# A two-block model on one core: matmuls of a recurrence spread over the array's four quarters, and four smaller edits of order

## The reference

```python
for l in range(DEPTH):                       # DEPTH = 2
    h = rmsnorm(x, norm1_g[l])
    p = h @ w_in[l]
    y_rw = rwkv7_branch(p_rw, ...)           # the recurrence
    y_ret = retention_branch(p_ret, cos, sin)
    y_sg = sgu_branch(p_sg, ...)
    ...
    x = x + jnp.sum(gates * proj, axis=2) @ w_out[l]
    x = x + conv_ffn(rmsnorm(x, norm2_g[l]), ...)
```

```python
# S_t = S_{t-1} (diag(w_t) - kk_t^T (a_t * kk_t)) + v_t^T k_t ;  y_t = S_t r_t
kk = kk / jnp.maximum(jnp.sqrt(jnp.sum(kk * kk, axis=-1, keepdims=True)), 1e-12)
```

```python
mixed = jnp.concatenate([rms_norm(c, conv_out_g[l]), rms_norm(a, attn_out_g[l])], axis=-1)
x = x + mixed @ w_out[l]
```

## Time and profile before

| | |
|---|---|
| median of 3 runs | 2949.22 us (2946.46 to 2950.34) |
| profiled execution, its time | 2951.45 us |
| its span in the profile | 2949.6 us |
| PE busy | 2849.4 us, 97% |
| DVE, ACT, POOL busy | 1443.0, 1100.2 and 1091.7 us |

### The profile page before, as it was taken

The page is one execution under the profiler, slowest core; times in us unless marked ns, Lnnn a source line. Parts: engine busy times, 40 slices in busy tenths (PEclk is TensorE's granted clock), DMA queues, the critical chain, the costliest instruction groups (busy, mean ns, idle before and its releaser), DMA issues. The chain is left out here.

```text
span 2949.6 us, 45829 instructions
## 1 busy us (share of the span) xinstructions
PE 2849.4 (97%) x19056; PEld 2164.1 (73%) x19057; DVE 1443.0 (49%) x1780; ACT 1100.2 (37%) x1609; POOL 1091.7 (37%) x627
## 2 busy tenths in 40 slices
PE   8998999999999999899999999999989989999997
PEld 7877878888888877797888888877767755444543
DVE  6276423468762526642336887259865231222223
ACT  5573242343332448324234333255564331111112
POOL 4264244445444436414444444434434230010000
PEclk9999999999999999999999999999989989999999
DMA  5220022222232422102222222222223147999995
GB/s 186 69 86 24 11 103 86 95 93 100 93 106 91 137 72 83 38 4 90 107 88 86 100 100 102 99 99 84 85 72 104 58 185 289 407 416 415 414 410 240
DMA packets 59194, 407.65 MB, mean 138 GB/s; under 512 B 9073, under 2 KB 9841, under 8 KB 19057
## 3 DMA queue, kind: packets, MB, share of 16 engines
q1 hardware_dynamic: 58992, 404.82, 36.5%
HBM read 397.45 MB, written 2.10 MB: 135 GB/s over the span
## 5 line engine op out<-in xcount | busy, mean ns | idle before, releaser
L1219 POOL TENSOR_TENSOR back_w_lo<-w,back_w_hi 128x1024 fp32r<-128x1024 f32 (+1 forms) x240 | 542.0, 2267 | 637.9 <-ACT back_w_hi L1380 637.7
L1380 ACT CAST back_w_hi<-w 128x1024 fp32r<-128x1024 f32 (+1 forms) x240 | 229.7, 957 | 511.4 <-PE bank L1235 502.9
L1230 PE MATMUL bank<-h_hi,back_w_hi 128*128 128x512 f32 x1072 | 268.5, 392 | 1.5 <-DVE back_made_lo L1565 1.5
L1235 PE MATMUL bank<-h_hi,back_w_lo 128*128 128x512 f32 x1072 | 264.7, 389 | 0.0
L1232 PE MATMUL bank<-h_lo,back_w_hi 128*128 128x512 f32 x1072 | 264.7, 389 | 0.0
L292 POOL TENSOR_TENSOR front_w_lo<-w,next_hi 128x1024 fp32r<-128x1024 f32 x68 | 178.3, 2625 | 225.4 <-ACT next_hi L476 225.4
L1230 PEld LDWEIGHTS bank<-h_hi,back_w_hi 128*128 128x128 f32 x1072 | 201.1, 188 | 47.4 <-issue 3.8
L1232 PEld LDWEIGHTS bank<-h_lo,back_w_hi 128*128 128x128 f32 x1072 | 201.2, 188 | 41.8
L1235 PEld LDWEIGHTS bank<-h_hi,back_w_lo 128*128 128x128 f32 x1072 | 201.2, 188 | 41.7
L3183 PE MATMUL bank<-moe_w,moe_hg 128*64 128x512 f32 x1024 | 226.1, 594 | 0.2 <-DMA moe_w<-in_moe_w 0.2
L1985 POOL TENSOR_TENSOR mid_w_lo<-w,mid_w_hi 128x1024 fp32r<-128x1024 f32 x60 | 149.1, 2489 | 188.9 <-ACT mid_w_hi L2436 188.5
(11 more groups left out here) (596 smaller groups left out, 5779.9 us busy)
## 6 DMA issues: line engine op xcount, KB each, us to landing
moe_w<-in_moe_w SPq DMA_DIRECT2D x128, 1024.0 KB, 13.3
moe_w<-in_moe_w SPq DMA_DIRECT2D x32, 2048.0 KB, 12.5
w<-in_ffn_up SPq DMA_DIRECT2D x44, 1024.0 KB, 4.8
w<-in_w_merge SPq DMA_DIRECT2D x22, 1536.0 KB, 6.2
w<-in_w_in SPq DMA_DIRECT2D x30, 1024.0 KB, 4.8
w<-in_w_mid SPq DMA_DIRECT2D x29, 1024.0 KB, 4.9
w<-in_ffn_down SPq DMA_DIRECT2D x16, 1408.0 KB, 6.0
w<-in_w_out SPq DMA_DIRECT2D x16, 512.0 KB, 4.0
```

The source lines that it names most:

```text
L1219: nc.gpsimd.tensor_tensor(split(B.w_lo, n), raw(n), split(B.w_hi, n).bitcast(F32), ALU.subtract).then_inc(f["w_lo"], 1)
L1230: nc.tensor.matmul(bank, B.w_hi[:, n % 2, k, :], x_hi[:, cols], start=start and k == 0, stop=False)
L1235: mm = nc.tensor.matmul(bank, B.w_lo[:, n % 2, k, :], x_hi[:, cols], start=False, stop=stop and k == len(hi) - 1)
L1380: nc.scalar.copy(split(B.w_hi, n), raw(n)).then_inc(f["w_hi"], 1)
```

## The change

1. Recurrence, first block: a set now holds two pairs of heads over all four chunks, where it held all four pairs over two chunks. In set 1 a head's tokens go to the other half of the partitions (`token_half`), so the products and transposes of both sets, issued in turn, fall on four quarters. The levels keep two. Products go to banks 0 to 2, ACT copies in turn between the sets, DVE runs both sets' LT first, subtracts for both sets before it transposes, and puts four of the masked products into the levels.
2. Recurrence, second block: `right`, `change` and `y` of both sets run as four quarters where reading and writing half differ. Where two quarters add to one place, PE waits for its own earlier sum (`part_done`). ACT copies set 0 and DVE set 1, DVE adds per set.
3. Front: `guard(2)` and `guard(3)` stand earlier in DVE's list.
4. The loop over layers is written out: the program holds both layers.
5. Mid: DVE's part of `early_a` goes from job 22 to 29, `norm_conv` from job 30 to 32 on both engines.

```diff
             betas(0)
+            guard(2)
             bias_group(0)
             bias_group(1)
             bonus(0)
             betas(1)
             bonus(1)
-            guard(2)
+            guard(3)
             betas(2)
             bonus(2)
-            guard(3)
             betas(3)
...
+    def token_half(s, h):
+
+        return heads[h ^ s]
...
+                def of(t, s, n, h):
+
+                    return t[heads[h], 2 * s + n % 2, chunk_tokens(4 * c + n // 2)]
+
+                def product(bank, lhs, rhs):
+                    for s, n, h in unit_order():
+                        mm = nc.tensor.matmul(T.ps[4 * s + bank][token_half(s, h), n * C:n * C + C], of(lhs, s, n, h),
+                                              of(rhs, s, n, h), start=True, stop=True)
...
+                    def add(kind, lhs, rhs, start, stop, which=(0, 1)):
+                        for i in range(2):
+                            for s in which:
+                                for h in range(2):
+                                    q = token_half(s, h) if kind in (RIGHT, SOLVED) else heads[h]
+                                    mm = nc.tensor.matmul(region(kind, s)[q, i * C:i * C + C], lhs(s, i, h),
+                                                          rhs(s, i, h), start=start and i == 0, stop=stop and i == 1)
...
+                    add(RIGHT, own(A.AkT, B.AkT), values, True, False).then_inc(rec["part_done"], 1)
+                    pe.wait_ge(rec["part_done"], 3 * n + 1)
+                    add(RIGHT, features(R.alpha), state, False, True).then_inc(rec["right_done"], 1)
+                    add(CHANGE, own(A.kT, B.kT), values, True, False)
+                    add(Y, values, own(A.AkrT, B.AkrT), True, False).then_inc(rec["part_done"], 1)
+                    for s in range(2):
+                        pe.wait_ge((rec["right_taken"], rec["right_taken_dve"])[s], n + 1)
+                        add(SOLVED, own(A.XT, B.XT), by_token(Rs), True, True, (s,)).then_inc(rec["u_done"], 1)
+                    pe.wait_ge(rec["part_done"], 3 * n + 2)
+                    add(Y, state, features(R.rho), False, False).then_inc(rec["part_done"], 1)
+                    add(CHANGE, own(A.bT, B.bT), by_token(Un), False, True).then_inc(rec["change_done"], 1)
+                    pe.wait_ge(rec["part_done"], 3 * n + 3)
+                    add(Y, by_token(Un), own(A.AbrT, B.AbrT), False, True).then_inc(rec["y_done"], 1)
...
+                    nc.vector.tensor_copy(of_set(Rs, 1), region(RIGHT, 1)).then_inc(rec["right_taken_dve"], 1)
...
-    with nc.Fori(0, DEPTH) as layer:
+    for layer in range(DEPTH):
...
-                if n == 22:
+                if n == 29:
                     early_a()
...
-                if n == 30:
+                if n == 32:
                     norm_conv()
```

More of the change, by code:

```diff
@@ L917, in _, with take_product @@
             def _(dve):
+                links = [Chain(dve, pre[s]["dve"]) for s in range(2)]
+                def take_product(s, n):
+                    B = sets[s]
+                    dve.wait_ge(pre[s]["products"], n + 2)
+                    nc.vector.tensor_tensor((B.AkT, B.AbrT, B.AkrT)[n][:, :, :], units(4 * s + n), mask(min(n, 1)),
+                                            ALU.mult).then_inc(pre[s]["masked"], 1)
                 for s, B in enumerate(sets):
-                    link = Chain(dve, pre[s]["dve"])
                     dve.wait_ge(pre[s]["products"], 1)
@@ new lines, in unit_order @@
+                def unit_order():
+                    return ((s, n, h) for n in range(U) for s in range(2) for h in range(2))
+                def of(t, s, n, h):
[4 more added lines that the diff above has]
+                                              of(rhs, s, n, h), start=True, stop=True)
+                        if n == U - 1 and h == 1:
+                            mm.then_inc(pre[s]["products"], 1)
@@ new lines, in turn @@
+                def turn(bank, src):
+                    for s, n, h in unit_order():
+                        mm = nc.tensor.matmul(T.ps[4 * s + bank][token_half(s, h), n * C:n * C + C], of(src, s, n, h),
+                                              T.ident[heads[h], heads[h]], start=True, stop=True)
+                        if n == U - 1 and h == 1:
+                            mm.then_inc(pre[s]["turned"], 1)
+                value = R.p[:, 8:12, :]
+                product(3, R.beta, R.alpha)
@@ L982, in _ @@
+                for bank, src in enumerate((R.beta, R.kappa, value)):
+                    turn(bank, src)
+                for bank, (lhs, rhs) in enumerate(((R.kappa, R.alpha), (R.beta, R.rho), (R.kappa, R.rho))):
+                    for s in range(2):
+                        pe.wait_ge(pre[s]["turned_taken"], bank + 1)
+                    product(bank, lhs, rhs)
                 for lev in range(LEVELS):
@@ L1015, in _ @@
             def _(pe):
-                for n, B, first, bank in steps:
-                    right, u, change, y = T.ps[bank:bank + 4]
+                for n in range(4):
                     now = chunk_tokens(4 * c + n)
-                    def add(out, lhs, rhs, start, stop):
-                        for j in range(PAIRS):
-                            for h, q in enumerate(heads):
-                                mm = nc.tensor.matmul(out[q, j * C:j * C + C], lhs(q, j), rhs(q, j),
-                                                      start=start and j == 0, stop=stop and j == PAIRS - 1)
-                        return mm
-                    own = lambda t: (lambda q, j: t[q, first + j, :])
-                    shared_by_chunks = lambda t: (lambda q, j: t[q, j, :])
-                    tokens = lambda t: (lambda q, j: t[q, j, now])
-                    if n >= 2:
-                        pe.wait_ge(rec["y_taken"], n - 1)
-                    add(right, own(B.AkT), own(B.vT), True, False)
+                    def add(kind, lhs, rhs, start, stop, which=(0, 1)):
[5 more added lines that the diff above has]
+                                                          rhs(s, i, h), start=start and i == 0, stop=stop and i == 1)
+                        return mm
+                    own = lambda a, b: (lambda s, i, h: (a, b)[s][token_half(s, h), 2 * n + i, :])
+                    by_token = lambda t: (lambda s, i, h: t[token_half(s, h), 2 * s + i, :])
+                    state = lambda s, i, h: M[heads[h], 2 * s + i, :]
+                    features = lambda t: (lambda s, i, h: t[heads[h], 2 * s + i, now])
+                    A, B = sets
+                    values = own(A.vT, B.vT)
+                    add(RIGHT, own(A.AkT, B.AkT), values, True, False).then_inc(rec["part_done"], 1)
@@ L1063, in _ @@
             def _(dve):
-                for n, B, first, bank in steps:
+                for n in range(4):
+                    dve.wait_ge(rec["right_done"], n + 1)
+                    nc.vector.tensor_copy(of_set(Rs, 1), region(RIGHT, 1)).then_inc(rec["right_taken_dve"], 1)
+                    dve.wait_ge(rec["u_done"], 2 * n + 2)
+                    nc.vector.tensor_scalar(of_set(Un, 1), region(SOLVED, 1), -1.0, None, ALU.mult).then_inc(
+                        rec["u_taken_dve"], 1)
                     dve.wait_ge(rec["change_done"], n + 1)
```

123 lines of the change are left out of this document (50 added, 73 removed).

## The result

The changed kernel takes 2921.02 us (median of 4; 2917.88 to 2923.03) where the kernel before takes 2949.78 in the same comparison: a ratio of 0.9906, 95% interval 0.9893 to 0.9918, so 28.8 us or 0.9% less. Run once more beside other kernels it gave 2920.70 and the same ratio, 0.9906 (0.9891 to 0.9920). The direction was forecast and the time lies just inside the wide range (2884 to 2922), but outside the forecast's own (2889 to 2903): the gain is little more than half of the 53 us forecast. It lies near rival 1 (2917), though the cause isn't rival 1's.

A forecast was written before the change was run, and what follows sets the result against it. PE's stream bounds the kernel (busy 2849.4 of 2949.6 us). Terms 12.6 + 7.7 + 4 + 2.4 + 18.8 - 2 + 10.4 = 53.9 gave 2896 us; own range 2889 to 2903, wide 2884 to 2922.

The forecast's parts named there:

- rival 1: Recurrence: quarters bring no gain, PE hands matmuls over at its present rate; 2917 us, chance 0.25.
- A: Front stage, both layers: earlier guards on DVE end PE's waits for `front_norm` and the low clock behind them; 12.6 us.
- B: Mid stage: without L2790 ahead, copies come 6.2 us earlier and PE's 8.23 us wait falls to about 2; 7.7 us.
- C: Mid stage: conv norm two jobs later ends PE's 3.8 us wait, about 2 to 3 us late next; 4 us.
- D: Start of layer 2: without the jump back PE's 4.05 us wait goes, POOL's low part then sets the start; 2.4 us.
- E: Recurrence, first part, four times: four quarters at 25 ns a matmul, levels at 3.85 us; 18.8 us, minus 2 for clock.
- F: Recurrence, second part, 16 steps: a chain of 3.48 us instead of 4.22, PE's fill-in groups fitting between; 10.4 us.
- rival 2: Mid stage: the stalls move only, so low parts and conv norm give 2 instead of 11.7; 2906 us, chance 0.12.

## Why the prediction was right in direction and too high in size

| term | forecast | measured in the profiles |
|---|---|---|
| A, guards | 12.6 | 5.7 + 6.2 = 11.9 |
| B, low parts | 7.7 | 3.4 |
| C, conv norm | 4 | 0.4 |
| D, layers written out | 2.4 | 1.8 |
| E and F, recurrence | 16.8 + 10.4 | 14.7 |

The terms are differences of two single profiles and carry the spread given with the table of stages. The forecast's own sum gives 2895.3, which it rounded up to 2896.

The wide range held because it took in rival 1, whose mechanism did not happen; that is luck. Two steps of the prediction carry most of the miss: E's rate of 25 ns and F's sum without packets (E and F together 12.5 us short of the forecast); then the durations taken for B and C (7.9).

**A** held: no wait for `front_norm`, and the window 217 to 233 is granted 1.00 where 0.50 stood in the earlier trace rows. **D** held: 0.32 us at the start of layer 2 and then a wait for POOL, as the rows of the changed kernel show (the 1.8 us gained are 3.7 less 1.83 that now stand in layer 2's front stage; for the same reason layer 2's share of A is 4.3 + 1.8 = 6.2, before rounding):

```profile
971.67 0.47 PE L361 MATMUL bank<-h_hi,next_hi 128*128 128x512 f32 x1 [0.32 <-PEq L1221]
...
974.21 2.11 PE L368 MATMUL bank<-h_hi,front_w_lo 128*128 128x512 f32 x8 [1.83 <-POOL front_w_lo L292]
```

**E** failed at "I take 25 ns, 11.2 us". The rate of the quarters was right, 15 ns, and rival 1 is refuted: PE hands matmuls over faster than every 29 ns. What I saw and sized wrongly were the packets. I wrote that each is used up in 1.9 us and one that is not there costs 2.26, and then chose a rate between 14.6 and 29 with no mechanism behind it. They are no occasional accident but the bound: 2.2 us from a transfer's start to its use, over 1 us before it starts, 27 ns a record. The prediction had named this as a sign of being wrong ("if instruction packets stall PE in E"). The groups took 14.6, 12.3, 12.8 and 12.5 us. The first level's end fell at 18.3, 17.1, 18.1 and 16.4 us where 14.3 was forecast and 21.3, 17.2, 21.0 and 17.3 stood before: 0.1 and 0.9 us gained in the two passes that had no pause before, and 3 in the two that had one, which is in part the end of that pause. The 14.3 was too early by the prediction's own rate as well: 11.2 us and a level's 128 matmuls at 29 ns, 3.7 us, make 14.9. The level's 3.85 was right where PE doesn't pause at a boundary, as the first of these two levels of the changed kernel shows, and 0.3 short where it does:

```profile
321.01:324.90 3.89, 3.89 (x132) 3.84 (x129) 3.17 (x5) 1.17 (x2) 2.51 (x2) 1.00 0.02 4
324.90:329.05 4.15, 4.15 (x130) 3.99 (x129) 3.17 (x5) 1.17 (x2) 2.51 (x2) 1.00 0.02 4
```

First parts together gave 11.4 us for 16.8 forecast, and 4.4 of them aren't the new code's: by so much the old first parts are shorter in the run with everything but the recurrence than in the profile of before. The clock's cost is in it: the profile has five stretches of 3.4 us at 0.50 in three of the four, two were there before.

**F** failed at "PE's fill-in groups fit between": its sum had no packet in it. The chain of 3.48 us a step was right (3.52 in the short passes), but a step has 258 records, one packet, so PE needs some 3.4 us for it whatever the chain does, and a transfer that starts late adds to the chain. Second parts gave 4.5 us instead of 10.4: 2.7 in each of two passes, and minus 0.8 and minus 0.1 in the others. Another 1.2 us, which the forecast did not have, went between the parts: a hand-over to the next block takes 1.1 us instead of 0.8.

**B** failed at "without them the copies are 6.2 us earlier". I priced L2790 by its length of 6.26 us and had its 2.1 us alone in my hands. The other 4 us belonged to POOL, and the two DVE operations with two operands in the state memory that came next paid them: 2.53 and 2.71 us instead of 0.68 and 0.69. PE's wait went from 8.23 to 5.58, not to 2. **C** failed in the same way at "about 2 to 3 us is late next": L2853 took 1.45 us for two before, L2889 takes 5.24, so that 3.6 us of wait and a second stretch of low clock came back. That is rival 2, given 0.12, for these two terms.

The terms make 32.2 of the 33.5 us between the two spans. By medians it is 28.8, since the profiled execution of the changed kernel was its shortest.

## What to carry to other kernels

Before pricing a faster matmul stream, divide its instructions by 256 and compare with the time that a packet takes (3.3 to 3.4 us at the least here); where the two are near, count no gain below it, and expect passes of equal code to differ by where the boundaries fall. When an operation is longer than its kind, find out whom it waits for before counting on its length: the length stays behind when the operation is moved. Edits that only change where code lies can interact; compare their sum with the whole.

## What was not expected of the hardware

- Eight small matmuls at the program's start change which passes stall hundreds of us later; with 80 of them, passes of 17.6, 14.1, 14.2 and 16.9 us became 14.1, 17.2, 17.2 and 14.3.
- The next transfer of instructions started 0.8 to 3.7 us behind a boundary in the changed kernel's recurrences and as early as 0.1 in those of the kernel before; where PE had paused for more than 0.2 us it was never sooner than 1.0 in any trace. It was latest where PE waited early in the packet, for the state or between two stages. What starts it is not settled: a wait for the state about 133 records behind a boundary went with a short pass, and one at 140 with a long one.
- A product of 64 x 64 on quarters that take turns starts every 15 ns. The Trainium skill, TensorEngine Tiling (Array Packing), section Restrictions and Gotchas, rules out row tiles in one PSUM bank at once. In these rows the two heads of a product read different row halves and write one bank, each its own half of the partitions, and they overlap. The Trainium skill, TensorE: Matmul & The Clock Gate, section Wait — 56ns, not 53.3ns?, gives about 25 ns as the least from start to start; the trace has 15.
- 80 such matmuls on one quarter at the program's start took 17 us, 107 ns a record.
